# Feed-forward products by Strassen's algorithm, and a layer norm without GpSimd, in a hybrid decoder layer

## The reference

```python
def layer_tail(x, ret_o, ret_gate, swa_o, w_out, ln_mix_g, ln_mix_b,
               w_ffn_gate, w_ffn_up, w_ffn_down, ln_ffn_g, ln_ffn_b):
    ret_o = head_group_norm(ret_o).astype(x.dtype) * jax.nn.silu(ret_gate)
    mixed = jnp.concatenate([ret_o.reshape(B, T, -1), swa_o.reshape(B, T, -1)], axis=-1)
    h = layer_norm(ALPHA * x + mixed @ w_out, ln_mix_g, ln_mix_b)
    f = (jax.nn.silu(h @ w_ffn_gate) * (h @ w_ffn_up)) @ w_ffn_down
    return layer_norm(ALPHA * h + f, ln_ffn_g, ln_ffn_b)
```

## Time and profile before

| | us |
|---|---|
| runs (3) | 2855.14, 2857.22, 2815.73; median 2855.14 |
| profiled execution, span | 2812.3 |
| TensorE busy | 2695.9 (96%) |
| VectorE busy | 1127.6 (40%) |
| ScalarE busy | 745.6 (27%) |
| GpSimd busy | 362.5 (13%) |
| DMA | 235.25 MB, mean 84 GB/s |

### The profile page before, as it was taken

One profiled execution on the slowest core, in us unless ns is written; L12 is line 12 of the kernel. 1 busy time (PEld: TensorE's weight loads), 2 busy tenths in 40 slices (PEclk: granted clock), 3 DMA queues, 4 the chain that ended last, 5 costly groups with the idle time before them and its releaser, 6 DMA issues.

```text
span 2812.3 us, 52158 instructions
## 1 busy us (share of the span) xinstructions
PE 2695.9 (96%) x19929; PEld 2618.7 (93%) x19929; DVE 1127.6 (40%) x1885; ACT 745.6 (27%) x1384; POOL 362.5 (13%) x318
## 2 busy tenths in 40 slices
PE   6999999999999996999999999999999999999993
PEld 5999999998778896999999999999999999999993
DVE  6334343434665457323333232323232323333346
ACT  4222222223443224322222222222222222222223
POOL 4102020202442178100000000000000000000002
PEclk9999999999999997999999999999999999999997
DMA  5324132322222221222222222222222222222231
GB/s 158 88 62 122 58 119 60 121 70 84 57 55 75 66 82 38 86 83 86 86 83 86 82 86 82 85 83 85 82 86 84 84 84 84 86 82 84 84 112 68
DMA packets 411228, 235.25 MB, mean 84 GB/s; under 512 B 14848, under 2 KB 404432, under 8 KB 409696
## 3 DMA queue, kind: packets, MB, share of 16 engines
q1 hardware_dynamic: 401936, 204.00, 25.1%
q0 software_dynamic: 8512, 25.08, 2.8%
q10 hardware_dynamic: 688, 4.85, 0.5%
HBM read 218.99 MB, written 15.34 MB: 83 GB/s over the span
## 4 chain that ended last, share of the span: by engine, by line
PE 90%; DVE 5%; ACT 2%; POOL 1%; issue 1%; DMA 1%; ACTq 0%; DVEq 0%; POOLq 0%
PE G L566 38%; PE G L577 20%; PE G L551 18%; PE G L591 7%; PE A L684 2%; PE A L704 1%; ACT lg L1142 1%; DVE ln_t L1669 1%; PE A L655 1%; DVE yo L1749 1%; DVE hl L1665 1%; DMA xin<-in_meta_tokens 1%; PE A L651 1%; POOL xl L1764 0%; PE A L756 0%
## 5 line engine op out<-in xcount | busy, mean ns | idle before, releaser
L1331 DVE TENSOR_TENSOR wl<-raw,wh 128x512 fp32r<-128x512 f32 x728 | 531.8, 732 | 1180.8 <-ACT wh L1014 1180.5
L1014 ACT CAST wh<-raw 128x512 fp32r<-128x512 f32 x760 | 470.5, 619 | 1472.8 <-PE G L566 571.5
L566 PE MATMUL G<-hh,wh 128*128 128x288 f32 x2752 | 579.2, 292 | 0.0
L566 PE MATMUL G<-hl,wh 128*128 128x288 f32 x2752 | 579.2, 292 | 0.0
L566 PE MATMUL G<-hh,wl 128*128 128x288 f32 x2752 | 579.2, 292 | 0.0
L566 PEld LDWEIGHTS G<-hh,wh 128*128 128x128 f32 x2752 | 437.4, 187 | 0.0
L566 PEld LDWEIGHTS G<-hl,wh 128*128 128x128 f32 x2752 | 437.4, 187 | 0.0
L566 PEld LDWEIGHTS G<-hh,wl 128*128 128x128 f32 x2752 | 437.4, 187 | 0.0
L551 PE MATMUL G<-xh,wh 128*128 128x288 f32 (+1 forms) x1344 | 308.3, 311 | 5.6 <-issue 4.1
L577 PE MATMUL G<-fh,wh 128*128 128x288 f32 x1408 | 297.1, 292 | 0.0
L577 PE MATMUL G<-fh,wl 128*128 128x288 f32 x1408 | 296.6, 292 | 0.0
(11 more groups left out here) (251 smaller groups left out, 2371.2 us busy)
## 6 DMA issues: line engine op xcount, KB each, us to landing
raw<-in_w_ffn_gate SPq DMA_DIRECT2D x176, 256.0 KB, 2.9
raw<-in_w_ffn_up SPq DMA_DIRECT2D x176, 256.0 KB, 2.9
raw<-in_w_ffn_down SPq DMA_DIRECT2D x176, 256.0 KB, 2.7
raw<-in_w_in SPq DMA_DIRECT2D x168, 256.0 KB, 2.9
raw<-in_w_out SPq DMA_DIRECT2D x64, 256.0 KB, 2.7
states<-in_state_ret POOLq DMA_DIRECT2D x32, 256.0 KB, 4.7
out_ret_s<-states POOLq DMA_DIRECT2D x32, 256.0 KB, 2.6
xin<-in_x_prompt ACTq DMA_DIRECT2D x4, 1024.0 KB, 8.5
```

Of the source, the lines that this page charges most:

```text
L566: mm = pe.matmul(G[:, par, n, 0:NL], w[:, q, k, :], x[:, kk, n * NL:(n + 1) * NL], start=one, stop=(kk == KT - 1 and w is wl))
L1014: act.copy(wh[:, q], raw[:, q]).then_inc(piece_hi, 1)
L1331: dve.tensor_tensor(wl[:, q], raw[:, q], f32(wh[:, q]), ALU.subtract).then_inc(piece_lo, 1)
```

## The change

The feed-forward products are done by a Strassen-like scheme (Winograd's form) on 2 x 2 blocks, 7 block products for 8.

Gate and up together are one product of weights of two block rows (gate, up) and two block columns (even k tiles, odd k tiles) with h of two block rows (even and odd rows) and two block columns (the token halves). A *quad* is one hidden tile of 128: it loads blocks a11, a12 (gate), a21, a22 (up) of 8 k tiles x 128 columns (512 KB each) and a second copy of a22 (`d22`), makes four weight combinations on VectorE (s1 to s4, 128x1024 each), and does seven products of 8 k x 3 terms = 24 matmuls of 128x288. Every product has its own high part (`w_hi`, ScalarE, five buffers) and low part (`w_lo`, VectorE, in place of the source; ten buffers, shared out in advance by `operand_homes`). SP's queue loads a block once the product that last used its buffer is done. h's seven combinations are made once, in the layer norm, as `X` (7 parts, high and low, 8 row pairs). Products collect in four regions of PSUM `G`; VectorE and ScalarE put the results together (U2, V, C11, C12, C21, C22) and make f's tiles.

All 44 quads of gate and up now run before any down product. Since f doesn't fit beside `X`, f's seven combinations (`fst`, made by VectorE for every second quad, split by ScalarE and VectorE) are written by GpSimd's queue to memory (`fd`), h too (`hd`). The down product takes 40 of the 44 hidden tiles in 5 groups of 8, each with 4 quads (each of 512 output columns): seven products of 24 matmuls, with f's combinations fetched into ten slots `F` (1.18 MB each) by GpSimd's queue, seven for a group. VectorE adds each product to one of the accumulators `acc`, `pacc`; h, fetched back, enters with ALPHA there. The 4 hidden tiles left over are multiplied the plain way at the end (`plain`, 384 matmuls), with the transposes in between.

In the layer norm, GpSimd's subtraction of the mean and its scaling by ALPHA are gone; VectorE subtracts the mean and multiplies by the reciprocal deviation for two rows at a time (both are read from PSUM `A`), makes four of the seven combinations (`tmp`) and all low parts; ScalarE applies the gain and makes the high parts. GpSimd only issues DMAs from there until the output's bias. TensorE does the first three products together, one row pair at a time as `X` comes.

The core of the diff:

```diff
+GROUP = 8
+D_GROUPS = HT // GROUP
+D_QUADS = 4
+PLAIN = HT - D_GROUPS * GROUP
...
+X_AT = (0, 1, 2, 3, 5, 6, 4)
+SRC_BUFS = (2, 3, 4, 5, 9, 10, 11, 12, 13, 14)
+HI_BUFS = (0, 1, 6, 7, 8)
+F_SLOTS = 10
...
-        hh, hl = at("hh", [P, KT, TL], R2, F32R), at("hl", [P, KT, TL], R3, F32R)
-        fh, fl = at("fh", [P, 2, KP, TL], R0, F32R), at("fl", [P, 2, KP, TL], R0 + RB // 2, F32R)
...
+        X = at("X", [P, 7, 2, 8, NL], XB, F32R)
+        F = at("F", [P, F_SLOTS, 2, 4, NL], XB, F32R)
...
+        hd = nc.dram_tensor("hd", [2, 2, D_QUADS, 2, P, NL], F32).ap()
+        fd = nc.dram_tensor("fd", [D_GROUPS, 7, P, 2, 4, NL], F32R).ap()
...
+            def load(key, src):
+                b, since, _ = HOMES[key]
+                if since >= 0:
+                    sp_.wait_ge(prod_done, since + 1)
+                elif b >= 6:
+                    rows_left(sp_, b)
...
+            for q in range(QUADS):
+                for what in ("a22", "a21", "a11", "a12", "d22"):
+                    load((q, what), block_of(q, what))
...
+            def part(n, k, s, bank, xh_, xl_, one, last):
+                h, l = wr[hi_buf(n)], wr[source(n)[0]]
+                for w, x, first, stop in ((h, xh_, one, False), (h, xl_, False, False), (l, xh_, False, last)):
+                    mm = pe.matmul(bank, w[:, k, :], x, start=first, stop=stop, skip_group_check=True)
...
+                return part(n, k, 0, banks[j], X[:, X_AT[j], 0, k, :], X[:, X_AT[j], 1, k, :], k == 0 and j < 4, k == 7)
...
+            for k in range(8):
+                pe.wait_ge(xw_lo, k + 1)
+                for n in range(3):
+                    if k == 0:
+                        pe.wait_ge(lo_done, n + 1)
+                    mm = gu_part(n, k)
+                    if k == 7:
+                        mm.then_inc(prod_done, 1)
...
+                    if t % D_QUADS == 0:
+                        pe.wait_ge(f_in[m % 4], 16 * (m // 4 + 1))
...
+                        pe.wait_ge(acc_done, 7 * t + (-2, -1, 0, -3, 1, 2, 3)[j])
...
+                if n > N_DN + 4:
+                    act.wait_ge(prod_done, N_DN + 2 * (n - N_DN - 4))
+                elif n > 5:
+                    act.wait_ge(prod_done, n - 4)
+                elif n > 2:
+                    rows_left(act, hi_buf(n))
+                elif n:
+                    act.wait_ge(piece_used, 4 * B_FFN)
+                act.copy(wr[hi_buf(n)][:, :, :], wf[source(n)[0]][:, :, :]).then_inc(hi_done, 1)
...
+            def s1(q):
+                here(q, "a22")
+                here(q, "a21")
+                dve.tensor_tensor(of(q, "a22"), of(q, "a22"), of(q, "a21"), ALU.add).then_inc(sums, 1)
...
+            def w_lo(n):
+                b_src = source(n)[0]
+                dve.wait_ge(hi_done, n + 1)
+                dve.tensor_tensor(wr[b_src][:, :, :], wf[b_src][:, :, :], f32(wr[hi_buf(n)][:, :, :]), ALU.subtract)\
+                    .then_inc(lo_done, 1)
...
+            def centre(i):
+                return dve.tensor_tensor(row_pair(i), row_pair(i), per_token(0), ALU.subtract)
+            def scale(i):
+                dve.tensor_tensor(row_pair(i), row_pair(i), per_token(2), ALU.mult).then_inc(normed, 1)
...
+                dve.tensor_tensor(X[:, 1:5, 1, i, :], tmp[:, i % 2, :, :], f32(X[:, 1:5, 0, i, :]), ALU.subtract)
+                dve.tensor_tensor(X[:, 5:7, 1, i, :], halves(yb[:, 2 * i + 1, :]), f32(X[:, 5:7, 0, i, :]), ALU.subtract)
+                dve.tensor_tensor(X[:, 0, 1, i, :], yb[:, 2 * i, 0:NL], f32(X[:, 0, 0, i, :]), ALU.subtract).then_inc(xw_lo, 1)
...
+                c.link(dve.tensor_tensor(x[:, 0:2, :], yb[:, 2 * i:2 * i + 2, NL:TL], halves(yb[:, 2 * i, :]), ALU.subtract))
+                c.link(dve.tensor_tensor(x[:, 2, :], yb[:, 2 * i + 1, NL:TL], x[:, 0, :], ALU.subtract))
+                dve.tensor_tensor(x[:, 3, :], yb[:, 2 * i + 1, 0:NL], x[:, 2, :], ALU.subtract).then_inc(xt_made, 1)
+                if i < 6:
+                    c.link(centre(i + 2))
+                    scale(i + 2)
+                if i:
+                    x_low(i - 1)
+                if i == 7:
+                    s4(0)
+                    w_lo(3)
+            x_low(7)
...
+                p = q // 2 - 1 if q % 2 == 0 else -1
+                if j == 0:
+                    finish_f(q - 1)
+                elif j == 1 and 0 <= p < 4 * D_GROUPS:
+                    ins = f_sums(p)
+                elif j == 4:
+                    dve.wait_ge(prod_done, n)
+                    dve.wait_ge(gu_act, act_at(q, M5_KEPT))
+                    dve.tensor_tensor(u2[:, :], u2[:, :], b_, ALU.add).then_inc(gu_dve, 1)
+                    dve.wait_ge(gu_dve, dve_at(q, U2_MADE))
+                    dve.tensor_tensor(vv[:, 1, :], u2[:, :], d_, ALU.add).then_inc(gu_dve, 1)
+                elif j == 6:
+                    dve.wait_ge(prod_done, n)
+                    dve.tensor_tensor(A[:, 3, 0:NL], u2[:, :], c_, ALU.add).then_inc(gu_dve, 1)
+                if j in (3, 4):
+                    next_sums(q, j)
+                if j == 5:
+                    next_sums(q, j)
+                if j == 1 and 0 <= p < 4 * D_GROUPS:
+                    c.link(ins)
+                w_lo(n + 2)
+                if j == 1 and 0 <= p < 4 * D_GROUPS:
+                    f_sums_2(p)
+                if j == 3 and p >= 0:
+                    f_low(p)
+                if j == 4:
+                    dve.wait_ge(gu_dve, dve_at(q, V_MADE))
+                    dve.tensor_tensor(vv[:, 1, :], vv[:, 1, :], A[:, 0, 0:NL], ALU.add).then_inc(gu_dve, 1)
+                if j == 6:
+                    next_sums(q, j)
+            def add_to(dst, t, j, bank, of_=None, first=False):
+                dve.wait_ge(prod_done, N_GU + 7 * t + j + 1)
+                src = bank[:, :, 0:NL]
+                if of_ is not None and t < D_QUADS and not first:
...
+                    ins = dve.scalar_tensor_tensor(out=dst, in0=dst, scalar=ALPHA, in1=src, op0=ALU.mult, op1=ALU.add)
+                elif first and t < D_QUADS:
+                    ins = dve.tensor_copy(dst, src)
+                else:
+                    ins = dve.tensor_tensor(dst, dst, src, ALU.add)
...
-            pool.wait_ge(mean_ready, 1)
-            for r in range(KT):
-                pool.tensor_tensor(yb[:, r, :], yb[:, r, :], mean[:, :], ALU.subtract).then_inc(centred, 1)
-            for r in range(KT):
-                pool.wait_ge(h_lo, r + 1)
-                pool.tensor_scalar(yb[:, r, :], yb[:, r, :], ALPHA, None, ALU.mult).then_inc(alpha_h, 1)
...
+                if m >= 4:
+                    pool.wait_ge(f_in[m % 4], 16 * (m // 4))
+                if m < F_SLOTS:
+                    pool.wait_ge(prod_done, N_GU - 7 + (0, 1, 2, 3, 6)[m // 2] + 1)
+                else:
+                    g0, j0 = (m - F_SLOTS) // 7, (m - F_SLOTS) % 7
+                    pool.wait_ge(prod_done, N_GU + 7 * (g0 * D_QUADS + D_QUADS - 1) + j0 + 1)
+                pool.dma_start(F[:, m % F_SLOTS], fd[g, X_AT[j]]).then_inc(f_in[m % 4], 16)
...
+                    pool.dma_start(fd[g, :, :, part_, k, :].rearrange("x p t -> p x t"), src[:, :, :]).then_inc(f_saved, 16)
...
+            for i, m in ((1, 4), (2, 5), (3, 6), (0, None)):
+                fetch_h(i, 0)
+                if m is not None:
+                    fetch(m)
+            save_pair(HT // 2 - 1)
+            for i in (1, 2, 3, 0):
+                fetch_h(i, 1)
+            for m in range(7, 7 * D_GROUPS):
+                fetch(m)
```

More of the change, by code:

```diff
@@ L122, in shape_constants, with operand_homes, home, source @@
     }
+def operand_homes():
+    free = [(-1, b) for b in SRC_BUFS]
+    loads = {b: 0 for b in SRC_BUFS}
+    homes = {}
+    def home(key, loaded, until):
+        since, b = min(free)
+        free.remove((since, b))
+        loads[b] += loaded
+        homes[key] = (b, since, loads[b])
+        free.append((until, b))
+    for q in range(QUADS):
+        for what, loaded, j in (("a22", 1, 1), ("a21", 1, 2), ("a11", 1, 0), ("s2", 0, 3), ("a12", 1, 4), ("s4", 0, 5), ("d22", 1, 6)):
+            home((q, what), loaded, 7 * q + j)
+    for n in range(N_DN, N_ALL):
+        home((n, "plain"), 1, n)
+    return homes
+HOMES = operand_homes()
+SRC_OF = ("a11", "a22", "a21", "s2", "a12", "s4", "d22")
+def source(n):
+    return HOMES[(n // 7, SRC_OF[n % 7])] if n < N_DN else HOMES[(n, "plain")]
+def hi_buf(n):
+    return HI_BUFS[(n - 1) % 5] if n else 15
 class Count:
@@ new lines, in gain @@
+            def gain(i):
+                act.wait_ge(normed, i + 1)
+                for r in (2 * i, 2 * i + 1):
+                    ins = act.activation(yb[:, r, :], yb[:, r, :], ACT.Identity, bias=vec[:, 3, r:r + 1], scale=vec[:, 2, r:r + 1])
+                ins.then_inc(h_made, 1)
+            gain(0)
+            for i in range(8):
+                if i < 7:
+                    gain(i + 1)
+                act.wait_ge(xt_made, i + 1)
+                act.copy(X[:, 1:5, 0, i, :], tmp[:, i % 2, :, :])
```

(11 more changed lines are left out.)

606 lines of the change are left out of this document (390 added, 216 removed).

## The result

The changed kernel takes 2680.82 us (median of four executions, 2677.78 to 2682.5) against 2854.97 for the kernel before: a ratio of 0.9402, 95% interval 0.9348 to 0.9456, so 174 us less. Beside later runs it came to 0.9386 (0.9369 to 0.9404) and 0.9409 (0.9351 to 0.9467). 2690 was forecast, with 2636 to 2745 as the range. One thing has to be said to read these numbers: the kernel before has times in two heaps, and the execution in its profile (span 2812.3) is from the small one, near 2815.73, while the changed kernel has one heap and its profiled execution (2682.45, span 2680.9) is an ordinary one. Much of what follows is about that.

The account below looks back on a forecast made before the run. TensorE's matmul pace was taken to bound the kernel: 2812.3 - 199.7 (matmuls) + 27 (layer norm) + 10 (DMA) = 2649.6, with 3.4 us around the span 2653, times 1.014 = 2690 us; range 2636 to 2745.

Parts of the forecast that it names:

- The matmuls: Feed-forward: 11,136 matmuls instead of 12,672, so 1536 fewer at 0.130 us each, -199.7 us.
- The price of 0.130 us: Feed-forward: each 128x288 matmul keeps its pace of 0.130 us, though 24 in a row add into one PSUM bank.
- The short case: Kernel before: six rows in a row into one bank of 256 columns, 4 taking 0.87 us, without a gap.
- The factor 1.014: Whole kernel: median of runs, 2855.14, over an execution like the profiled one; scales 2653 to 2690 us.
- +27: Layer norm: steady pace 8.7 us later, 122 matmuls less in hand (15.9), 2 to 3 us at half pace.
- 18.4 and 18.7 us a quad: VectorE's work per gate/up and down quad, hidden under TensorE's 21.84 us, costing nothing on the path.
- +10 of 0 to 32: DMA stalls in the down product and at the change from gate/up: +10 us taken, nearer the low end.
- The burst: Down groups' last quads: f's fetches leave weights little for 22 us; three bursts cost 0 to 17 us.
- the change of stage: Gate/up to down: 7 fetches, 4.7 MB of h and weights meet in some 55 us, costing 0 to 15 us.
- The first rival: Down product: mixed DMA traffic flows slowly and starves weights, 92 us a group instead of 87.4; 2735 us, chance 15%.
- three signs of being wrong: TensorE under 95% busy in the down stage, a low part releasing TensorE, or a matmul pace not 0.130.
- the main case: Whole kernel: TensorE-paced with small stalls, 2636 to 2715 us, likeliest 2690; chance 75%.

## Why the prediction was right, and where it was not

**The matmuls.** 7392 + 2304 + 1440 = 11,136 are in the page, as counted. The price of 0.130 us is the term that was mis-sized: the changed kernel runs at 0.1330 in every profile of it. The short case in the earlier trace rows could not have told: its 256 columns take 0.22 us a matmul, at a granted clock of 1.00 (290 to 292 us), against 0.130 for 288, so it is another pace altogether. 11,064 x 0.0030 = 33 us more than the sum had; its 2653 for an execution like the profiled one met 2682.45.

**The factor 1.014.** The step from 2653 to 2690 said that what the other executions have more is not in the trace, and scaled it. It isn't a share of all work. It is the pace of the feed-forward: 41 us of the kernel before's ordinary executions, and the changed kernel has it in all of its own. So the 37 us that the factor added are the 33 that the price left out, by luck of size. Made for ordinary executions of both, the sum needs no factor: 1536 x 0.1333 = 205 less, and the other terms below.

**The layer norm.** +27 was forecast. In the profile the eighth step of 9 matmuls starts 70.1 us after the last out-projection start and ends 72.4 after it; before, 63.2 us from that start held 194 matmuls. That is 9.2 us later, 122 matmuls less in hand at 0.133 (16.2) and about 1 at the low clock: 26.4. The forecast worked this out from rows without GpSimd beside them, and those held. What it didn't separate the run of the move alone did: the move to VectorE gives 6 us back, so that Strassen's operands and the small stock of products, by difference, cost some 32.

**VectorE.** 18.4 and 18.7 us a quad forecast, 17.5 and 17.6 measured (78 and 79% of 22.3). Its idle time ends on TensorE, as said; the margin is shown.

**DMA.** +10 of 0 to 32. The burst came as described (3.7 to 14.8 us) and cost 0 of its 0 to 17; the change of stage cost 4.7 to 6.9 of its 0 to 15. The forecast took the sharing of the queues from a row of 21 packets to 162 and held it to be worse for the weights than an even exchange. In the burst they moved 1094 to 612, 1.09 of 6.16 MB, which is better than even: that step was too dark. Of the +10 some 5 came, all at the change of stage. The first rival did not occur, and the doubled traffic shows that it stood near.

**Not in the sum.** The out-projection ended 6.5 us later than in the profile before; its last matmul starts at 1073.9 to 1080.7 us in the profiles of the changed kernel and its variants, and at 1074.1 and 1079.1 in the two of the kernel before, so this is no effect of the change. The tail, from the last feed-forward matmul, is 1.3 us shorter.

Together, profile against profile: -199.7 + 33 + 26.4 + 4.7 + 6.5 - 1.3 = -130.4; the spans differ by 131.4. Ordinary against ordinary: -205 + 26.4 + 5 - 1.3, and 11,064 x 0.0003 = 4 less since 133.0 is below 133.3, is -179; the medians of the last runs differ by 176 to 179.

**Its own signs.** Two of the three signs of being wrong came: the pace is 0.133, not 0.130, and at the change of stage a low part (wr, L1855) releases TensorE, though for 4 us in all. The third did not: TensorE is busy throughout in the down product. One sum does not come out: the upper end of the main case, 2715, is 2723 by its own terms (2812.3 - 199.7 + 37 + 32 + 3.4, times 1.014); the range isn't touched.

What stays open: what a stream's start must be like to fall into the rhythm of 130.0 ns, and whether the changed kernel's products have one. The traces hold one clue and no more: of ten starts after a pause in the layer norms of the kernel before and its variants (at the upper clock level from the first matmul on), the two whose second matmul came 212 ns after the first went into 130.0, the eight with 206 to 209 ns into 133.3.

## What to carry to other kernels

Before a pace from a profile is multiplied by thousands, ask whether the profiled execution stands for the median; where it doesn't, look for one line that runs at two paces in that very trace (here the tail gave 0.1333 for the line that had 0.130). A move of work is judged at the prices that hold once the disturber has gone, and one part of a change done alone tells which part costs. A transfer's landing time is to be held against the lead with which its buffer was freed: landings of 14.8 to 16.7 us against leads of 16 to 19 cost TensorE nothing, and twice the traffic cost some 14 us a group.

## What was not expected of the hardware

Matmuls of 128x288, each with its own weight load, ran for 80 us and more at 130.0, 132.1, 132.5, 133.0, 133.3 or 136.6 ns, all at the full granted clock and with TensorE waiting for nothing. The same lines had 130.0 in the kernel before and 133.3 in the run of the layer norm alone, and one order with the same buffers had 132.1 and 136.6 in two kernels. The Trainium skill's page "TensorE: Matmul & The Clock Gate" (Wait — 56ns, not 53.3ns?) gives, for matmuls back to back, the columns over 2.4 GHz and some 2.5 ns: an estimate by it is 122.5 ns for 288 columns. It speaks there of no weight load for each matmul, which all of these have, and no stretch of any run here reached it.
